# The key and value ring in the order of use, and the streams' bias rows issued from ScalarE's queue, in a two-layer streaming encoder

## The reference, cut to what matters

```python
def fox_sample(q, k, v, logf, ck, cv, clogf):
    fq = jnp.cumsum(logf, axis=1)
    c_after = lax.cumsum(clogf, axis=1, reverse=True) - clogf
    fk = jnp.concatenate([-c_after, fq], axis=1)
    kk = jnp.concatenate([ck, k], axis=1)
    vv = jnp.concatenate([cv, v], axis=1)
    s = jnp.einsum('bihd,bjhd->bhij', q, kk) * (D ** -0.5)
    s = s + fq.transpose(0, 2, 1)[..., :, None] - fk.transpose(0, 2, 1)[..., None, :]
    s = jnp.where(valid, s, -jnp.inf)
    p = jax.nn.softmax(s, axis=-1)
    return jnp.einsum('bhij,bjhd->bihd', p, vv)
```

## Time and profile before

| | |
|---|---|
| three runs | 2954.14, 2959.53, 2959.44 us; median 2959.44 |
| profiled execution, its own time | 2958.0 us |
| its span, first to last instruction | 2956.2 us |
| busy in the span | TensorE matmul 93%, weight load 87%, GpSimd 36%, ScalarE 23%, VectorE 23% |
| DMA | 293.82 MB, mean 99 GB/s |
| band attention | from 775.5 to about 851 us |
| fox attention | from 2044.8 to about 2407 us |

### The profile page before, as it was taken

One profiled execution on the slowest core, in us unless ns is written; L12 is line 12 of the kernel. 1 busy time (PEld: TensorE's weight loads), 2 busy tenths in 40 slices (PEclk: granted clock), 3 DMA queues, 4 the chain that ended last, 5 costly groups with the idle time before them and its releaser, 6 DMA issues.

```text
span 2956.2 us, 46765 instructions
## 1 busy us (share of the span) xinstructions
PE 2744.2 (93%) x19779; PEld 2583.3 (87%) x19779; DVE 681.7 (23%) x1442; ACT 688.4 (23%) x913; POOL 1055.3 (36%) x403
## 2 busy tenths in 40 slices
PE   7999999999789999999999999997655689999997
PEld 7999999998579999999999999996322269999997
DVE  4110123323533110123110113211221223110112
ACT  2221222210342221222221222211332232221221
POOL 3443444330343443443443443321221233443442
PEclk9999999996799999999999999998777789999998
DMA  3222212212442222212222212225677742212211
GB/s 130 71 68 89 71 59 85 72 43 109 164 158 72 71 68 89 71 59 84 73 73 82 71 61 68 104 94 187 213 217 228 222 158 73 71 68 86 74 55 66
DMA packets 55200, 293.82 MB, mean 99 GB/s; under 512 B 8321, under 2 KB 12178, under 8 KB 28978
## 3 DMA queue, kind: packets, MB, share of 16 engines
q1 hardware_dynamic: 55090, 292.24, 29.4%
HBM read 279.95 MB, written 12.27 MB: 99 GB/s over the span
## 4 chain that ended last, share of the span: by engine, by line
PE 86%; DMA 8%; DVE 2%; SPq 1%; ACT 1%; POOL 1%; issue 1%; DVEq 0%; ACTq 0%; POOLq 0%
PE ps L312 74%; DMA kv_ring<-in_fox_kc 8%; PE ps L676 4%; PE ps L973 1%; PE ps L1006 1%; PE ps L947 1%; PE ps L932 1%; POOL w_lo L298 1%; SPq L903 1%; PE ps L1262 0%; PE ps L1251 0%; DVE sq_sum L1692 0%; PE ps L378 0%; PE ps L979 0%; PE ps L1237 0%
## 5 line engine op out<-in xcount | busy, mean ns | idle before, releaser
L298 POOL TENSOR_TENSOR w_lo<-w_raw,w_hi 128x2048 fp32r<-128x2048 f32 (+2 forms) x185 | 792.6, 4285 | 688.7 <-ACT w_hi L293 680.4
L312 PE MATMUL ps<-xn_hi,w_hi 128*128 128x320 f32 x3616 | 829.6, 311 | 18.4 <-POOL w_lo L1632 11.0
L312 PE MATMUL ps<-xn_lo,w_hi 128*128 128x320 f32 x3616 | 826.4, 310 | 0.0
L312 PE MATMUL ps<-xn_hi,w_lo 128*128 128x320 f32 x3616 | 825.9, 310 | 0.0
L312 PEld LDWEIGHTS ps<-xn_hi,w_hi 128*128 128x128 f32 x3616 | 606.3, 189 | 20.6 <-POOL w_lo L1632 11.0
L312 PEld LDWEIGHTS ps<-xn_lo,w_hi 128*128 128x128 f32 x3616 | 607.7, 189 | 0.0
L312 PEld LDWEIGHTS ps<-xn_hi,w_lo 128*128 128x128 f32 x3616 | 606.8, 188 | 0.0
L293 ACT ACTIVATE w_hi<-w_raw 128x2048 fp32r<-128x2048 f32 (+2 forms) x185 | 326.7, 1766 | 535.5 <-PE ps L312 466.7
L565 POOL TENSOR_TENSOR h_lo<-prod,h_hi 128x640 f32 x88 | 139.2, 1581 | 713.7 <-ACT h_hi L518 713.7
L312 PE MATMUL ps<-h_hi,w_hi 128*128 128x320 f32 x1408 | 321.0, 309 | 0.0
L312 PE MATMUL ps<-h_lo,w_hi 128*128 128x320 f32 x1408 | 320.8, 309 | 0.0
(11 more groups left out here) (196 smaller groups left out, 1895.9 us busy)
## 6 DMA issues: line engine op xcount, KB each, us to landing
w_raw<-in_w_up SPq DMA_DIRECT2D x87, 1024.0 KB, 4.9
kv_ring<-in_fox_kc SPq DMA_DIRECT2D x32, 1024.0 KB, 13.6
kv_ring<-in_fox_vc SPq DMA_DIRECT2D x32, 1024.0 KB, 12.0
w_raw<-in_w_down_a SPq DMA_DIRECT2D x32, 768.0 KB, 4.2
w_raw<-in_w_in SPq DMA_DIRECT2D x24, 1024.0 KB, 4.9
w_raw<-in_w_down_b SPq DMA_DIRECT2D x32, 640.0 KB, 3.9
kv_ring<-in_band_kc SPq DMA_DIRECT2D x8, 1024.0 KB, 5.9
kv_ring<-in_band_vc SPq DMA_DIRECT2D x8, 1024.0 KB, 8.2
```

The lines of the kernel that those rows point to most:

```text
L298: nc.gpsimd.tensor_tensor(out=w_lo[:, slot, 0:cols], in0=w_raw[:, slot, 0:cols], in1=w_hi[:, slot, 0:cols].bitcast(F32), op=ALU.subtract). ...
L312: last = nc.tensor.matmul(ps[:, 2 * unit + half, 0:HALF], w_part[:, slot, w:w + P], a_part[:, k, half * HALF:(half + 1) * HALF], start=k = ...
```

## The change

Three things:

- The chunks are numbered in the order of use: keys of 0, keys of 1, values of 0, keys of 2, values of 1, ... The load of chunk c still waits for chunk c - 5. SP issues in this order. Each chunk of keys now counts as used by itself (a new semaphore sk_used, raised by its own last matmul).
- The bias rows of unit n + 2 are issued from ScalarE's queue, in s_copy_probs of part c of unit n, right after ScalarE's wait for the last transpose of n. SP still issues those of units 0 and 1.
- The prompt's bias of pair (n + 3) // 2 is issued after the values of unit n (n odd), before it was that of pair n // 2 (n even).

```diff
+        def chunk_of(self, n, ch, values):
+            if values:
+                return self.chunks * min(2 * n + 2, 2 * self.units - 1) + ch
+            return self.chunks * max(2 * n - 1, 0) + ch
+
         def place_of(self, n, ch, values):
-            c = 2 * self.chunks * n + (self.chunks if values else 0) + ch
+            c = self.chunk_of(n, ch, values)
             return c % RING, 16 * (c // RING + 1)
 
         def chunk_used(self, eng, c):
-            n, at_ = divmod(c, 2 * self.chunks)
-            if at_ < self.chunks:
-                eng.wait_ge(self.slogits_ready, n + 1)
+            at_, ch = divmod(c, self.chunks)
+            if at_ == 0 or (at_ % 2 == 1 and at_ < 2 * self.units - 1):
+                eng.wait_ge(self.sk_used, self.chunks * ((at_ + 1) // 2) + ch + 1)
             else:
-                eng.wait_ge(self.sv_used, self.chunks * n + at_ - self.chunks + 1)
+                n = self.units - 1 if at_ == 2 * self.units - 1 else at_ // 2 - 1
+                eng.wait_ge(self.sv_used, self.chunks * n + ch + 1)
...
-        def load_sample_bias(self, sp, n):
-            if n >= 2:
-                sp.wait_ge(self.spt_ready, len(self.parts) * (n - 1))
+        def load_sample_bias(self, eng, n):
             for cols, src in self.loads["sample_bias"](n):
-                sp.dma_start(self.tiles["s_s"][n % 2][:, cols], src).then_inc(self.sbias_loaded[n % 2], 16)
-
-        def sp(self, sp, ahead):
+                eng.dma_start(self.tiles["s_s"][n % 2][:, cols], src).then_inc(self.sbias_loaded[n % 2], 16)
+
+        def sp(self, sp, keys_given, values_given):
...
+            keys, values = (1, 0) if self.chunks == 2 else (3, 1)
             for n in range(self.units):
-                if n >= 2:
-                    self.load_sample_bias(sp, n)
-                if n >= ahead:
-                    self.load_keys(sp, n)
+                if self.chunks == 2 and keys_given <= n + keys < self.units:
+                    self.load_keys(sp, n + keys)
+                if values_given <= n + values < self.units:
                     for ch in range(self.chunks):
-                        self.load_values(sp, n, ch)
-                if n >= 4 and n % 2 == 0:
-                    self.load_prompt_bias(sp, n // 2)
+                        self.load_values(sp, n + values, ch)
+                if self.chunks == 1 and n + keys < self.units:
+                    self.load_keys(sp, n + keys)
+                if n % 2 == 1 and n + 3 < self.units:
+                    self.load_prompt_bias(sp, (n + 3) // 2)
...
                     for p in range(4):
-                        nc.tensor.matmul(ps[32 * p:32 * p + 32, 4 + ch, 0:512], qz_s[:, n % 2, p, :],
-                                         kv_ring[r][:, p, :], start=True, stop=True)
+                        last = nc.tensor.matmul(ps[32 * p:32 * p + 32, 4 + ch, 0:512], qz_s[:, n % 2, p, :],
+                                                kv_ring[r][:, p, :], start=True, stop=True)
+                    last.then_inc(self.sk_used, 1)
...
             def s_copy_probs(n, part):
                 act.wait_ge(self.spt_ready, steps * n + list(parts).index(part) + 1)
+                if part == "c" and n + 2 < self.units:
+                    self.load_sample_bias(act, n + 2)
                 if part == "a" and n:
                     act.wait_ge(self.so_ready, n)
...
                 for n in (0, 1):
                     band.load_keys(sp, n)
-                    band.load_values(sp, n, 0)
+                band.load_values(sp, 0, 0)
+                band.load_keys(sp, 2)
+                band.load_values(sp, 1, 0)
...
-                band.sp(sp, ahead=2)
+                band.sp(sp, keys_given=3, values_given=2)
...
                 fox.load_keys(sp, 0)
                 sp.dma_start(outs["fox_v"][:, :, early:], vc[:, :, early:]).then_inc(kv_odd_stored, 16)
-                fox.load_values(sp, 0, 0)
-                fox.load_values(sp, 0, 1)
-                fox.sp(sp, ahead=1)
+                fox.load_keys(sp, 1)
+                fox.sp(sp, keys_given=2, values_given=0)
```

More of the change, by code:

```diff
@@ L830, in __init__ @@
             self.sprobs_ready, self.spt_ready, self.spt_copied = s("sprobs_ready"), s("spt_ready"), s("spt_copied")
-            self.sv_used, self.so_ready = s("sv_used"), s("so_ready")
+            self.sk_used, self.sv_used, self.so_ready = s("sk_used"), s("sv_used"), s("so_ready")
             self.sinv_done, self.so_scaled = s("sinv_done"), s("so_scaled")
@@ L883, in load_keys @@
                 r, _ = self.place_of(n, ch, False)
-                self.ring_wait(sp, 2 * self.chunks * n + ch)
+                self.ring_wait(sp, self.chunk_of(n, ch, False))
                 sp.dma_start(kv_ring[r][:, :, :], self.loads["keys"](n, ch)).then_inc(self.ring_loaded[r], 16)
@@ L888, in load_values @@
             r, _ = self.place_of(n, ch, True)
-            self.ring_wait(sp, 2 * self.chunks * n + self.chunks + ch)
+            self.ring_wait(sp, self.chunk_of(n, ch, True))
             sp.dma_start(kv_ring[r][:, :, :], self.loads["values"](n, ch)).then_inc(self.ring_loaded[r], 16)
```

## The result

Three runs of the changed kernel took 2869.80, 2874.36 and 2874.75 us, median **2874.36 us** against 2959.44: ratio 0.9714, 95% interval 0.9691 to 0.9736. The span of the profiled execution is 2872.6 us (before 2956.2).

What follows compares the result with a forecast made beforehand. Band was held bound by TensorE, fox by keys requested without lead, then by DMA work. 2958.0 - 77.9 (fox) + 1.0 (band) = 2881.1, with 1.4 us from profile to median 2882 us; range 2840 to 2930.

Steps and rivals of the forecast that it cites:

- The bound before: In fox, keys were requested with zero uses of lead, leaving the flight of bias and 2 MB of keys open; 22.7 us a unit.
- 17.9 us a unit: Fox's new pace, set by DMA work: 16.8 mean, plus 1.5 late half, minus 0.6 restart, plus 0.2 holes.
- The range: Span around the 2882 us sum: 2865 to 2900 us, with holes at 0 to 1.3 us a unit in fox.
- The end of fox: Output projection starts at 2331.4 instead of 2409.26, 9.2 us after the last values land; gain 77.9 us.
- What is late next: After the change, TensorE in fox waits for the landing of values, not keys; no size given.
- ScalarE's issues in fox: Bias issues put 1.2 us ahead of each part c copy, 17 us in all, covered and so counted as nothing.
- Band, 1 us: Bias issues from ScalarE in band, where TensorE has no slack, cost 1 us, bounds 0 and 2.
- SP's waits: Prompt bias's wait for the last maxima delays keys some 5 us, costing nothing; key and value load waits short, in both.
- Rivals 1 and 2: Two queues hinder each other in fox: 24.2 us a unit, 2977 us, chance 0.06; by half, 21.0, 2930 us, 0.18.
- Rival 3: Alternating spreads the bias, fox's slow stretch disappears; TensorE and ScalarE bound at 15.2 us a unit, 2842 us; chance 0.14.
- Rival 4: Fox's keys are late because of rate, not request; nothing moves, 2959 us; chance 0.03.
- VectorE: Sign of being wrong: VectorE waiting for bias rows would mean they land more than a unit after issue.

Runs made afterwards that it cites:

- e2: The changed kernel with the bias rows issued by SP again instead of from ScalarE's queue: 2873.32 us.
- e3: The kernel before, with the old ring order, only the bias rows moved to ScalarE's queue: 2906.74 us.
- e1: The changed kernel itself run again, beside other runs on one chip: 2874.31 us.
- e4: The changed kernel with each bias row of fox stored twice in DRAM, so a load has 16 rows, each to 8 partitions: 2834.41 us.
- f4: The changed kernel with fox's bias rows stored 16 times, so a load reads 128 different rows in one block: 2805.33 us.
- f1: The kernel before (old order, bias rows from SP) with each bias row of fox stored twice, for 16 x 8 loads: 2915.27 us.
- f3: The changed kernel with the prompt's bias loaded one pair later: 2872.03 us.
- f2: e4 with the bias rows issued from SP's queue instead of ScalarE's: 2838.37 us.
- g2: f4 with each head's prompt bias row also stored 128 times (4 MB more) ahead of fox: 2822.42 us.
- h2: g2 with only pairs 2 to 7 of the prompt's rows stored (3 MB), after fox's first bias loads: 2801.61 us.
- g1: f4 with room for 17 copies of each row, so loads are 8 x 16 again, of different rows: 2871.72 us.
- h1: f4 with two stores of 8 copies each in room for 9, so loads are 16 x 8, of different rows: 2832.24 us.

## Why the prediction was right, step by step

Forecast 2882 us, measured 2874.36; the case called likeliest (0.59) happened, and the gain lies where it was put, in fox.

- **The bound before** (a lead of zero uses, the bias rows ahead of the keys): right. e2 takes the new order without ScalarE's queue and gains all; e3 takes only the queue and gains 50 us. The prediction held that the whole flight of bias and keys lay open; the 3.5 us a unit of e3 are the bias's part of it.
- **17.9 us a unit**: measured 17.38, in e1 16.92, so the term was too large by 0.5 to 1.0. The mean work was put at 16.8 less 0.6 for the restart, 16.2 us, with a share of 0.9 over fox; measured is a share of 0.95, and 0.95 x 17.38 = 16.5 us. On top came 1.5 us for the late half and 0.2 for holes. If the late half works all of the 17.38 us it is 0.9 above the mean, and nothing is left for holes. By this reckoning the lead of the late half is what was mis-sized. That a late half exists fits the shares of about a half, and that it is eight engines is what e4 bears out: with 16 the unit falls by 2.8 us. That these are the same eight each time no view shows. The 2.8 us are more than the 0.9 that levelling alone would give, since packets of 8 KB beside the bias also got shorter (478 and 434 ns).
- **The range** given beside the sum, 2865 to 2900 with holes of 0 to 1.3 us, is wrong at its lower end: without holes the sum gives 17.7 us a unit and 2879. The measured time lies under that and over 2865, for the reason just given and not for want of holes.
- **The end of fox**: predicted 2331.4, measured 2327.82. ScalarE takes the slab at 2321.08, predicted 2324.7, and the 6.74 us from there were predicted as 6.7. Of the 3.6 us, the 15 units give 7.8 too early, the later first keys 1.3 and the last unit 2.9 the other way; that the two cancel a part of the 7.8 is luck. Gain 81.4 us, predicted 77.9; 2.1 us more came behind fox, which nothing in the sum covers.
- **What is late next**: the landing of the values, as predicted, 35.5 us against 16.3 for keys. With the bias rows on SP (e2) it is the keys, 49.3 us against 16.4, so this depends on the queue.
- **ScalarE's issues in fox**: each takes its time (0.58 us twice, ahead of the copy; a few 1.15 to 1.17), and it costs nothing that shows: e1 is e2. The cover was said to be 17.9 - 15.2 = 2.7 us. It is larger, since f4 runs at 12.8 us a unit with the same issues. The "14.0 us of TensorE's own work" was partly read at the lower clock (mean 0.73 over fox before, 0.95 in f4) and held waits for other engines.

```profile
2202.14 0.58 ACTq L907 DMA_DIRECT2D fox_s_s<-after_dram  x1
2202.76 0.58 ACTq L907 DMA_DIRECT2D fox_s_s<-neg_f_dram  x1
2203.39 0.28 ACT L1061 ACTIVATE fox_s_pt<-ps 128x128 f32<-128x128 f32 x1 [0.76 <-issue]
```

- **Band, 1 us**: not settled. The output projection behind it starts at 856.57, before at 855.73, and from band's first keys to there 81.35 us go by for 80.22. But f1, whose band is that of the kernel before, took 81.62 us, and e2, with the rows on SP, 81.31: one profile doesn't resolve 1 us here. An issue takes 0.33 us, as put, and the place can be seen: a pair in the middle takes 17.18 us as before (17.19), and in the first one the issue at 782.20 (0.40 us) delays the copy by as much (782.65, before 782.25), with the next keys still at the lower clock.
- **SP's waits**: that for the last maxima counted as nothing, right by f3. Those for places are in both loads, as predicted, but not all short, up to 11.0 us; f3 has 65 us more of them at the same time.
- **Rivals 1 and 2** (two queues in each other's way): didn't happen; e1 and e2, and e4 and f2, are within each other's intervals. The Trainium skill's rule that a second queue brings no bandwidth ("DMA: Bandwidth & Descriptors", "Issuing engines are not separate DMA queues") agrees with both; that the queue gains 50 us under the old order is a matter of what waits behind what.
- **Rival 3** (the slow stretch goes by itself, 15.2 us a unit, 2842): didn't happen; 206 to 256 GB/s still stand at a full share. And its floor was too high, as f4 shows.
- **Rival 4** (rate and not request): no, though after the change rate is the bound.
- **VectorE** waited in L1137 for bias rows 4 times, 15.8 us in all, the longest 6.7. The prediction took that as a sign against it, that they land more than a unit after their issue. The sign did appear, in a few units, and costs nothing: e2 has no such wait in fox and the same time.

## What to carry to other kernels

Number a ring's places by the order in which they are used. A load that waits for the use just ahead of its own has no lead, however many places there are, and a chain of waits that names the landing together with a DMA share well under 1 is how it shows. Once the transfers are the bound, look for stretches at half the share (too few engines in some load) and at full share with low GB/s, and try 128 rows in one block for every load in them, even if a small table must be stored 16 times over: here this was worth 69 us on top of the change's 85, 40 of them by using all engines. And store it where nothing stands behind it in the queue (g2 against h2).

## What the runs showed of the hardware beyond what was expected

- The form of a 512 KB load sets the pace of all traffic beside it: 8 x 16, 16 x 8 and 128 rows, all of different data, gave 297 GB/s (g1), 354 (h1) and 402 (f4) over fox, and packets of 8 KB beside it took 471, 431 and 317 ns. The Trainium skill ("DMA: Bandwidth & Descriptors", "Rules for kernel authors") asks for an outermost dimension that is a multiple of 16, ideally the 128 partitions; the step from 16 to 128, 1.8 us a unit, agrees with the "ideally". The packet of 4 KB takes 250 ns in the first two forms and 165 in the last.
- Reading a row 16 times instead of once cost nothing that can be told from the 0.5 us a unit between two profiles of one kernel (17.4 and 16.9, g1 17.0), 8 times nothing (e4 and h1 14.6). It had looked like the cause until g1 and h1; a run that comes out at the expected side doesn't show its reason if its edit changes two things.
- An issue on SP takes 0.3 to 0.9 us mostly, but 8.99 us behind an 8 MB store (f4; 8.98 in g2) and 24.26 us behind a further 4 MB (g2).
